# A hybrid decoder layer on one core: in the joint stretches a unit's three plain splits move ahead of its last sums on VectorE

## The reference, cut to what matters

```python
h = rms_norm(x, pre_norm_w[l])
proj = h @ w_in[l]
...
qa, za, ga, kc, vc, ksl, vsl, kw, vw, qb, kb, vb, zb = jnp.split(proj, splits, axis=-1)
...
ob = dilated_mixer(to_heads(qb, N_HEADS_B), to_heads(kb, N_HEADS_B), to_heads(vb, N_HEADS_B), positions)
...
x = x + rms_norm(mix @ w_out[l], post_norm_w[l])
```

## Time and profile before

| what | value |
|---|---|
| median of 3 runs | 1745.94 us (1745.61 to 1745.96) |
| the profiled execution, its time | 1746.14 us |
| its span, first to last instruction | 1744.3 us |
| granted TensorE clock, mean | 1.000 |
| TensorE matmuls busy | 1736.8 us, 100% of the span |
| VectorE busy | 1359.5 us, 78% |
| ScalarE busy | 953.4 us, 55% |
| GpSimd busy | 608.2 us, 35% |

### The profile page before, as it was taken

The page is one execution under the profiler, slowest core; times in us unless marked ns, Lnnn a source line. Parts: engine busy times, 40 slices in busy tenths (PEclk is TensorE's granted clock), DMA queues, the critical chain, the costliest instruction groups (busy, mean ns, idle before and its releaser), DMA issues.

```text
span 1744.3 us, 22634 instructions
## 1 busy us (share of the span) xinstructions
PE 1736.8 (100%) x7791; PEld 1436.0 (82%) x7791; DVE 1359.5 (78%) x1419; ACT 953.4 (55%) x1292; POOL 608.2 (35%) x834
## 2 busy tenths in 40 slices
PE   9999999999999999999999999999999999999998
PEld 8888888888888888888888888888888888888886
DVE  7657666787887878996769666966696796979797
ACT  7644445554554546476537553755365664646554
POOL 3335303368494857822432242334233330000000
PEclk9999999999999999999999999999999999999999
DMA  8866677555564555566655666566556566656575
GB/s 293 251 204 191 195 230 242 179 161 180 158 191 157 172 167 170 180 202 192 187 180 198 193 189 188 193 198 188 184 181 212 171 186 230 208 191 239 181 280 216
DMA packets 181822, 344.78 MB, mean 198 GB/s; under 512 B 14944, under 2 KB 19296, under 8 KB 181216
## 3 DMA queue, kind: packets, MB, share of 16 engines
q1 hardware_dynamic: 181008, 342.58, 61.4%
q10 hardware_dynamic: 720, 0.93, 0.1%
HBM read 339.27 MB, written 4.19 MB: 197 GB/s over the span
## 4 chain that ended last, share of the span: by engine, by line
PE 92%; DVE 5%; issue 2%; ACT 1%; ACTq 0%; DVEq 0%
PE acc L777 20%; PE acc L783 20%; PE acc L780 20%; PE acc L909 7%; PE acc L910 7%; PE acc L911 7%; DVE w_parts L1645 1%; PE acc L1024 1%; PE heads L911 1%; PE heads L910 1%; PE heads L909 1%; DVE sum L2110 1%; DVE w_parts L2303 1%; PE trans L910 0%; PE trans L909 0%
## 5 line engine op out<-in xcount | busy, mean ns | idle before, releaser
L1645 DVE TENSOR_TENSOR w_parts<-raw,w_parts 128x1024 fp32r<-128x1024 f32 x510 | 653.1, 1282 | 316.7 <-ACT w_parts L1217 315.1
L1217 ACT ACTIVATE w_parts<-raw 128x1024 fp32r<-128x1024 f32 x510 | 538.6, 1058 | 475.3 <-PE acc L783 393.9
L777 PE MATMUL acc<-w_parts,x_parts 128*128 128x512 f32 x1536 | 601.6, 392 | 0.0
L783 PE MATMUL acc<-w_parts,x_parts 128*128 128x512 f32 x1536 | 598.3, 390 | 0.0
L780 PE MATMUL acc<-w_parts,x_parts 128*128 128x512 f32 x1536 | 598.1, 389 | 0.0
L783 PEld LDWEIGHTS acc<-w_parts,x_parts 128*128 128x128 f32 x1536 | 288.5, 188 | 61.1
L780 PEld LDWEIGHTS acc<-w_parts,x_parts 128*128 128x128 f32 x1536 | 288.7, 188 | 58.5
L777 PEld LDWEIGHTS acc<-w_parts,x_parts 128*128 128x128 f32 x1536 | 288.7, 188 | 58.2
L909 PE MATMUL acc<-w_parts,x_parts 128*128 128x512 f32 x629 | 245.3, 390 | 0.2
L910 PE MATMUL acc<-w_parts,x_parts 128*128 128x512 f32 x629 | 245.0, 389 | 0.0
L911 PE MATMUL acc<-w_parts,x_parts 128*128 128x512 f32 x629 | 244.8, 389 | 0.0
(11 more groups left out here) (365 smaller groups left out, 2078.9 us busy)
## 6 DMA issues: line engine op xcount, KB each, us to landing
raw<-in_w_in SPq DMA_DIRECT2D x478, 512.0 KB, 3.5
blocks_raw<-in_w_out SPq DMA_DIRECT2D x96, 512.0 KB, 4.7
raw<-in_w_out SPq DMA_DIRECT2D x32, 512.0 KB, 4.2
raw<-in_w SPq DMA_DIRECT2D x16, 512.0 KB, 4.5
x_tok<-in_x SPq DMA_DIRECT2D x4, 1024.0 KB, 8.1
xt_raw<-in_x_t SPq DMA_DIRECT2D x7, 512.0 KB, 5.9
wpost<-in_post_w SPq DMA_DIRECT2D x4, 512.0 KB, 5.5
out<-y SPq DMA_DIRECT2D x4, 512.0 KB, 2.7
```

Source lines behind the costliest of these rows:

```text
L777: nc.tensor.matmul(o, stat_hi, mov_hi, start=(k == 0), stop=False)
L783: last = nc.tensor.matmul(o, stat_lo, mov_hi, start=False, stop=(k == KB - 1))
L1217: nc.scalar.activation(w_hi[:, n % SPLIT_SLOTS, :, 0:width], raw[:, n % RAW_SLOTS, :, 0:width], ACT.Copy).then_inc(hi_ready, 1)
L1645: V.tensor_tensor(w_lo[:, s, :, 0:width], raw[:, n % RAW_SLOTS, :, 0:width], w_hi[:, s, :, 0:width].bitcast(F32), ALU.subtract).then_inc(l ...
```

## The change

VectorE's sums of a unit are cut in two functions. `unit_sums_13` now stands behind the half split of position m+1, and `unit_sums_24` behind the split of m+2, so that each of the three splits goes ahead. VectorE's order in a unit becomes: split(m), half split(m+1), first sums, split(m+2), last sums, two rests, split(m+3). Since the last sums still read the raw blocks of m and m+1, SyncE's load of position m+4 into the slot of m now waits for the last sums (`sums_24_made`) in place of split(m); the loads behind it on the queue stay behind it.

```diff
                 for m in range(2 * PAIRS):
                     n, j = joint_place(m)
                     first = sp.snap((VB if j else KBC) + NC * g)
-                    sp.wait_ge(lo_ready, 16 * (C_B + 1 + 4 * g) + m - RAW_SLOTS + 1)
+                    if m - RAW_SLOTS in JOINT_UNITS:
+                        sp.wait_ge(sums_24_made, N_JOINT * g + JOINT_UNITS[m - RAW_SLOTS] + 1)
+                    else:
+                        sp.wait_ge(lo_ready, 16 * (C_B + 1 + 4 * g) + m - RAW_SLOTS + 1)
...
-            def unit_sums(c, m, i, g):
-
-                unit_no = N_JOINT * g + i
+            def unit_blocks(m):
+                blocks_in = raw[:, :, :, :].rearrange(by_unit)
+                one = 2 * (m % RAW_SLOTS)
+                return (blocks_in[:, one:one + 4:3, :], blocks_in[:, one + 2:one + 3, :],
+                        blocks_in[:, one + 1, :], blocks_in[:, one + 3, :])
+
+            def unit_sums_13(c, m, i, g):
+
+                b11_b22, b12, _, _ = unit_blocks(m)
                 for at in (m, m + 1):
                     dve.wait_ge(raw_landed[at % RAW_SLOTS], 16 * (PAIRS // RAW_SLOTS * c + at // RAW_SLOTS + 1))
                 if i > 0:
-                    dve.wait_ge(sums_13_ready, unit_no)
...
+                    dve.wait_ge(sums_13_ready, N_JOINT * g + i)
                 V.tensor_tensor(sum_13[:, :, :], b12.broadcast_to([P, 2, NC]), b11_b22, ALU.subtract).then_inc(sums_13_made, 1)
+
+            def unit_sums_24(m, i, g):
+
+                unit_no = N_JOINT * g + i
+                _, _, b21, b22 = unit_blocks(m)
                 dve.wait_ge(sums_13_made, unit_no + 1)
                 if i > 0:
                     dve.wait_ge(sums_24_ready, unit_no)
...
-                    if m in JOINT_UNITS:
-                        unit_sums(c, m, JOINT_UNITS[m], g)
                     if m - 1 in JOINT_UNITS:
                         split_half(c, m)
+                        unit_sums_13(c, m - 1, JOINT_UNITS[m - 1], g)
                     else:
                         split(c, m)
                     if m - 2 in JOINT_UNITS:
+                        unit_sums_24(m - 2, JOINT_UNITS[m - 2], g)
                         unit_rests(JOINT_UNITS[m - 2], g)
```

## The result

The changed kernel takes 1752.82 us (median of 6 runs, 1751.89 to 1753.13) against 1745.95 us before (6 runs, 1745.61 to 1746.35): a ratio of 1.0039, 95% interval 1.0028 to 1.0049. It is **6.9 us slower**. I had forecast 1751.3, slower, in a range of 1744 to 1757.

The account below looks back on a forecast made before the run. TensorE was taken as the bound, busy all the time. Each stretch would lose 2.07 us (stalls 1.35, restarts 0.33, slower pace 0.39) against 0.72, so +5.4 us for four: 1751.3 us, range 1744 to 1757.

Parts of the forecast that it names:

- The mechanism: Joint units: stall at position 8 goes; later refill delays transpose 0.8 us, and ScalarE, without idle time, delays later splits.
- the load of position 8 was never to be the last to arrive in unit 1: Sign of being wrong, unit 1: the prediction fails if position 8's load isn't the last to arrive there.
- The stalls: TensorE in units 1 to 3: 0.55 us each at positions 14 and 18, 0.1 at 15, 0.15 at 19.
- from position 20 on the moves end and ScalarE and VectorE run ahead again: Behind the units: positions 20 to 31 don't change, so no loss was counted there.
- The ceiling of 2.9 us: Most that can be won: 4 x 0.72 us, from position 8's stall and restart (0.33) and slower pace behind (0.39).
- Rival 1: Stall at position 8 goes, ScalarE and VectorE absorb 0.8 us in units 2 and 3: 1743.1 us; chance 0.10.
- rival 4: Whole kernel: gains and losses cancel, nothing measurable, 1745.9 us; chance 0.25 together with rival 2.
- Rival 2: Refill hidden, only reordering costs: no stall at 14, about 0.5 at 18, 1747.5 us; chance 0.25 with rival 4.
- Rival 3: Loads slower, 4.8 us for each burst's first; 10, 11, 14, 18 late: 1755 to 1763 us; chance 0.15 above 1754.

Follow-up runs that it names:

- x_sums: The changed kernel, but its sums read four resident blocks of x instead of the raw weight blocks, and loads again wait for split(m) alone: 1747.57 us.
- not_last: The changed kernel with the change in units 0 to 2 only; unit 3 has the old order and position 20's load waits for split(16): 1758.47 us.
- unit1_only: The kernel before, but in unit 1 only split(8) goes ahead of the sums and position 12's load waits for the last sums: 1744.41 us.
- light_unit1: Only split(8) moved ahead of unit 1's sums, as against the kernel before, plus VectorE's plain-position splits in the units making one block's rests: 1744.47 us.
- copy_first: The changed kernel, but ScalarE rounds the last sums behind copy(m+3) instead of ahead of it: 1753.73 us.

## Why the prediction was right, and where it was off

- **The mechanism held.** On the old scale (1.42 taken off) the transpose started at 937.12 where I had worked out 937.1, copy(14) at 942.70 (942.7), split(14) ended at 945.02 (945.0) and split(18) at 956.04 (955.95). The load of position 8 was issued 4.1 us later than before (4.5 foreseen) and cost nothing at position 8 itself. One of the signs of being wrong was badly put: the load of position 8 was never to be the last to arrive in unit 1. It landed at 929.5, that of 10 at 932.5, in the order that the prediction itself had worked out.
- **The stalls** at 14 and 18 measured 0.46 and 0.47 for 0.55 each, at 15 and 19 together 0.13 for 0.25. The units thus lost a little less than worked out. The 135 matmuls from the first to the last `trans` row took 32.21 us for 32.7; of those 32.7 some 0.26, the stall at 19 and its restart, lie behind the last row.
- **The step that failed: "from position 20 on the moves end and ScalarE and VectorE run ahead again".** Unit 3 delays the loads of 20 to 22. In the trace copy(22) waits for its load, VectorE's sums of the extra results stand behind split(22), ScalarE scales them ahead of copy(23), and split(23) is late: stalls of 0.19, 0.18, 0.07 and 1.38 us, and 0.11 for each restart, 2.3 us in all. In the fourth stretch the load of 22 took 6.7 us. x_sums and not_last have none of it. The sum had put this term at nothing. Without it the four stretches lost 4.5 us, for the 5.4 of the sum; so the forecast of the time came as near as it did partly by luck, as the units were put too high by 0.9 where 2.3 was left out.
- **The ceiling of 2.9 us was too high.** I took the pace of 0.230 for a consequence of the stall; unit1_only and light_unit1 show it isn't, as it stays without the stall (0.38 us a stretch). It stands in both kernels, so the difference of the two didn't suffer.
- **Rival 1** (nothing follows) and **rival 4** fell. **Rival 2** (only the order costs) describes x_sums, whose loads come early enough for it: 1747.57 for the 1747.5 given there. The change isn't that kernel. **Rival 3** was right in kind, not in size: the first load of a burst took 3.4 to 3.7 us, not 4.8, and the third 5.2 to 6.7. The slowest of these, the load of 22 in the fourth stretch, goes with the longest stall, 1.38 at 23; the 6.2 of position 14 in the third stretch cost nothing that shows (a stall of 0.47 like the others).
- VectorE's 1.85 us of gaps in unit 0 cost split(7) 0.2 us. That agrees with the rule of the Trainium skill's page "SBUF — State Buffer", section "SBUF: two separate sides": the two engines lock a shared port pair, one for a whole instruction while the other waits. It doesn't prove an exclusive lock: a shared port of which either engine gets all while the other is idle isn't told apart from it by any run here.
- ScalarE kept its written order: the moves and copy(15) stood behind the rounding that waited 1.61 us. By the Trainium skill's page "TensorE: Matmul & The Clock Gate", section "Architectural detail: the array is 16× 32×32, not 1× 128×128", ScalarE's and VectorE's queues are strictly first in, first out; this trace agrees. But copy_first shows that taking ScalarE's wait away isn't a gain by itself.

## What to carry to other kernels

When an operation is moved behind others, look at what it reads, and not only at what it makes: here the last reader of a buffer moved back by 4 us, and without the refill's wait 5.3 of the 6.9 us lost were gone. Put ahead only the one split that is late, and leave the last reader where it is: that version (unit1_only) came out 1.3 us under the kernel before, with an interval that just reaches no change, and one split ahead in every unit already loses. And follow a delay past the stage that made it, to the next place where three engines hand work to one another.

## What the runs showed of the hardware that I had not expected

In not_last, fourth stretch, TensorE stood idle for 1.91 us at position 16 and then ran on at half clock for a while. Four windows of the profile (width, busy us and number of instructions of PE, PEld, DVE, ACT and POOL, granted clock, DMA share, GB/s):

```profile
1316.00:1318.00 2.00, 0.58 (x3) 0.50 (x4) 2.00 (x4) 2.00 (x3) 0.00 (x0) 1.00 0.07 26
1318.00:1320.00 2.00, 2.00 (x7) 1.58 (x6) 2.00 (x2) 1.94 (x4) 0.00 (x0) 0.56 0.66 164
1320.00:1322.00 2.00, 2.00 (x7) 1.59 (x6) 2.00 (x3) 1.95 (x3) 0.00 (x0) 0.58 1.05 406
1322.00:1324.00 2.00, 2.00 (x11) 1.63 (x10) 2.00 (x3) 1.58 (x3) 0.00 (x0) 1.00 0.87 249
```

The granted clock went from its upper level, 2.4 GHz, to the lower, 1.2 GHz: it is 0.56 and 0.58 as a mean of the second and third window, in which a matmul came every 0.43 us instead of 0.227 for some 3.4 us, and was back at 1.00 by 1322. In the three other stretches TensorE stood idle for 1.78, 1.78 and 1.98 us at the same place, once longer than here, with no such effect; the step of that unit was 1.5 to 1.7 us longer in the fourth stretch than in them. So a stall can cost more than its own length, and its length alone didn't decide it. That kernel's runs spread over 5 us where those of the other experiments spread over 0.5 to 3.2, and its fastest run had a mean granted clock of 1.000, its slowest 0.997. That the clock makes all of this spread is not shown; only one of its runs has a trace.
